# Where the high and low halves of weights and activations start in SBUF: rows placed by their byte address modulo 256

## What is computed

```python
def first_block(x, ...):
    for layer in range(2):
        h = rms_norm(x, g_mix[layer])
        x = x + (even_mixer(h, ...) if layer == 0 else odd_mixer(h, ...))   # projections in, attention, projection out
        h = rms_norm(x, g_mlp[layer])
        x = x + jnp.square(jax.nn.relu(h @ w_up[layer])) @ w_down[layer]    # 1024 -> 4096 -> 1024
    return x
# then x = x + mlstm_mixer(rmsnorm(x), ...), x = x + nsa_mixer(rmsnorm(x), ...), and a last rmsnorm
```

## The kernel before

| kind | moving, before | loaded beside it | offset before | moving, after | loaded beside it | offset after |
|---|---|---|---|---|---|---|
| narrow, h moving, 256 columns | h 192 | w 128 | 192 | h_hi 64, h_lo 0 | w_hi 128, w_lo 64 | 64 |
| MLP up L1164, 512 | h pair 192 | w_lo 128 | 192 | h pair 64 | w_lo 64 | 0 |
| MLP up L1165, 256 | h 192 | w_hi 128 | 192 | h 64 | w_hi 128 | 64 |
| MLP down, 512 | w 128 | u 64 | 192 | w_hi 128, w_lo 64 | u_hi 128, u_lo 64 | 0 |
| wide, h stationary, 512 | w 128 | h 192 | 64 | as above | h_hi 128, h_lo 64 | 0 |
| values of the last mixer (48 of the wide ones) | w 128 | h 192 | 64 | as above | h_hi 64, h_lo 0 | 192 |
| even_y stationary, 512 | w 128 | 128 | 0 | as above | y_hi 128, y_lo 64 | 0 |
| odd_y, nsa_y stationary | w 128 | 96, 64 | 224, 192 | as above | as above | 0 |
| ml_y stationary, 512 | w 128 | hi 160, lo all residues | 32, all | as above | as above | 0 |
| one chunk, w moving, h stationary, 256 | w 128 | h 192 | 64 | as above | h_hi 128, h_lo 64 | 0 |

## Time and profile before

### The profile page before, as it was taken

The page is one execution under the profiler, slowest core; times in us unless marked ns, Lnnn a source line. Parts: engine busy times, 40 slices in busy tenths (PEclk is TensorE's granted clock), DMA queues, the critical chain, the costliest instruction groups (busy, mean ns, idle before and its releaser), DMA issues.

```text
span 949.1 us, 14124 instructions
## 1 busy us (share of the span) xinstructions
PE 940.5 (99%) x5608; PEld 794.3 (84%) x5608; DVE 627.3 (66%) x1134; ACT 561.6 (59%) x926; POOL 98.3 (10%) x142
## 2 busy tenths in 40 slices
PE   9999999999999999999999999999999999999997
PEld 7777888888888777688888888999988889988876
DVE  6767687764446565568776354677479757677875
ACT  6697555553434776655554343556477547777774
POOL 0210000000000000000000007145002201311101
PEclk9999999999999999999999999999999999999999
DMA  9733455565554425146555556233333644421201
GB/s 366 311 130 129 171 222 177 183 216 177 178 203 152 169 97 178 45 138 221 190 197 187 185 212 217 90 133 134 134 133 104 229 171 178 169 99 45 90 23 45
DMA packets 22417, 152.59 MB, mean 161 GB/s; under 512 B 2512, under 2 KB 2768, under 8 KB 4944
## 3 DMA queue, kind: packets, MB, share of 16 engines
q1 hardware_dynamic: 21424, 148.25, 43.4%
q0 software_dynamic: 640, 3.15, 1.0%
q10 hardware_dynamic: 288, 0.30, 0.1%
HBM read 150.64 MB, written 1.05 MB: 160 GB/s over the span
## 4 chain that ended last, share of the span: by engine, by line
PE 96%; DVE 2%; ACT 1%; DMA 1%; issue 0%; SPq 0%; ACTq 0%; DVEq 0%
PE bank L188 20%; PE bank L190 20%; PE bank L189 20%; PE bank L1164 13%; PE bank L1165 6%; PE bank L930 2%; PE bank L2313 1%; PE bank L2322 1%; PE bank L954 1%; PE bank L2337 1%; PE bank L1600 1%; PE bank L943 1%; PE bank L760 1%; PE bank L1585 1%; PE bank L1577 1%; DMA raw<-in_chunks 1%
## 5 line engine op out<-in xcount | busy, mean ns | idle before, releaser
L158 DVE TENSOR_TENSOR w_hi_lo<-raw,w_hi_lo 128x2048 fp32r<-128x2048 f32 x121 | 277.5, 2296 | 138.2 <-ACT w_hi_lo L154 138.0
L154 ACT ACTIVATE w_hi_lo<-raw 128x2048 fp32r<-128x2048 f32 x135 | 257.6, 1911 | 108.8 <-PE bank L190 108.3
L1164 PE MATMUL bank<-h,w_hi_lo 128*128 128x512 f32 x512 | 181.2, 396 | 0.0
L1165 PE MATMUL bank<-h,w_hi_lo 128*128 128x256 f32 x512 | 144.4, 282 | 0.0
L188 PE MATMUL bank<-h,w_hi_lo 128*128 128x256 f32 x448 | 129.5, 289 | 0.1
L189 PE MATMUL bank<-h,w_hi_lo 128*128 128x256 f32 x448 | 125.2, 279 | 0.0
L190 PE MATMUL bank<-h,w_hi_lo 128*128 128x256 f32 x448 | 125.0, 279 | 0.0
L1164 PEld LDWEIGHTS bank<-h,w_hi_lo 128*128 128x128 f32 x512 | 96.2, 188 | 23.4 <-issue 0.2
L190 PE MATMUL bank<-w_hi_lo,mlp_u_lo 128*128 128x512 f32 x256 | 100.6, 393 | 0.0
L188 PE MATMUL bank<-w_hi_lo,mlp_u_hi 128*128 128x512 f32 x256 | 100.5, 393 | 0.0
L189 PE MATMUL bank<-w_hi_lo,mlp_u_hi 128*128 128x512 f32 x256 | 99.7, 390 | 0.0
(11 more groups left out here) (402 smaller groups left out, 1588.3 us busy)
## 6 DMA issues: line engine op xcount, KB each, us to landing
raw<-in_chunks SPq DMA_DIRECT2D x136, 1024.0 KB, 4.8
even_bias<-in_even POOLq DMA_DIRECT2D x8, 384.0 KB, 3.4
xres<-in_x SPq DMA_DIRECT2D x2, 512.0 KB, 5.3
raw<-in_chunks SPq DMA_DIRECT2D x2, 512.0 KB, 6.2
ml_z<-in_ml SPq DMA_DIRECT2D x1, 896.0 KB, 6.5
small<-in_small SPq DMA_DIRECT2D x1, 559.5 KB, 11.6
final_gain<-in_fnorm SPq DMA_DIRECT2D x1, 512.0 KB, 3.3
out<-final_xn SPq DMA_DIRECT2D x1, 512.0 KB, 2.6
```

The lines of the kernel that those rows point to most:

```text
L154: act.activation(w_hi[slot][:, :], raw[slot][:, :], ACT.Copy).then_inc(hi_ready, 1)
L158: dve.tensor_tensor(w_lo[slot][:, :], raw[slot][:, :], w_hi[slot][:, :].bitcast(F32), ALU.subtract).then_inc(lo_ready, 1)
L1164: pe.matmul(dst[:, :], w_hi[slot][:, cols], h[:, k, :, :], start=(k == 0), stop=False)
L1165: last = pe.matmul(dst[:, 0:S], w_lo[slot][:, cols], h[:, k, 0, :], start=False, stop=(k == KT - 1))
```

## The change

No instruction is added, removed or moved: engine by engine the program has the same instructions with the same shapes and the same waits in the same order. Only the SBUF addresses differ. The weights' ring becomes one tensor in which w_lo starts at 64 modulo 256 and w_hi at 128. h becomes a room that is read through three views: as pairs at 64 for the MLPs (`hu_hi`, `hu_lo`), as two planes at 128 and 64 where it is stationary (`h_hi`, `h_lo`), and as two planes at 64 and 0 for the mLSTM and the last mixer (`hm_hi`, `hm_lo`). Unused pads move u and y so that their high half starts at 128 and their low half at 64.

```diff
-    w_both = [sb(ctx, f"w_hi_lo{i}", [P, 2, CHUNK], F32R) for i in range(RING)]
-    w_hi, w_lo = ([w[:, x, :] for w in w_both] for x in range(2))
+    SHIFT = 16
+    W_ROW = CHUNK + 3 * SHIFT
+    W_SLOT = 2 * CHUNK + 4 * SHIFT
+    w_room = sb(ctx, "w_hi_lo", [P, RING * W_SLOT + 2 * SHIFT], F32R)
+    w_both = [w_room[:, i * W_SLOT:i * W_SLOT + 2 * W_ROW].rearrange("p (x c) -> p x c", x=2) for i in range(RING)]
+    w_hi, w_lo = ([w[:, x, 0:CHUNK] for w in w_both] for x in range(2))
...
+    sb(ctx, "pad_h", [P, 64])
...
             self.u_hi = sb(stack, f"{name}_u_hi", [P, D_FF // P, S], F32R)
+            sb(stack, f"{name}_pad_lo", [P, 3 * SHIFT])
             self.u_lo = sb(stack, f"{name}_u_lo", [P, D_FF // P, S], F32R)
...
-                pe.matmul(dst[:, :], w_hi[slot][:, cols], h[:, k, :, :], start=(k == 0), stop=False)
-                last = pe.matmul(dst[:, 0:S], w_lo[slot][:, cols], h[:, k, 0, :], start=False, stop=(k == KT - 1))
+                pe.matmul(dst[:, :], w_hi[slot][:, cols], h_pairs[:, k, :, :], start=(k == 0), stop=False)
+                last = pe.matmul(dst[:, 0:S], w_lo[slot][:, cols], hu_hi[:, k, :], start=False, stop=(k == KT - 1))
...
-    h = sb(big, "h", [P, KT, 2, S], F32R)
-    h_hi, h_lo = h[:, :, 0, :], h[:, :, 1, :]
+    PLANE = KT * S
+    h_room = sb(big, "h", [P, 2 * PLANE + 4 * SHIFT], F32R)
+
+    def plane(at):
+        return h_room[:, at:at + PLANE].rearrange("p (k s) -> p k s", k=KT)
+
+    h_pairs = h_room[:, 0:2 * PLANE].rearrange("p (k x s) -> p k x s", k=KT, x=2)
+    hu_hi, hu_lo = h_pairs[:, :, 0, :], h_pairs[:, :, 1, :]
+    h_hi, h_lo = plane(SHIFT), plane(PLANE + 4 * SHIFT)
+    hm_hi, hm_lo = plane(0), plane(PLANE + 3 * SHIFT)
...
+    sb(es, "pad_even_y", [P, 48])
     ey_hi = sb(es, "even_y_hi", [P, KT, S], F32R)
+    sb(es, "pad_even_lo", [P, 3 * SHIFT])
...
-            self.y_lo = sb(stack, "ml_y_lo", [P, ML_TILES, KW], F32R)[:, :, KW - S:KW]
+            sb(stack, "pad_ml_lo", [P, 3 * SHIFT])
+            self.y_lo = sb(stack, "ml_y_lo", [P, ML_TILES, S], F32R)
...
-                last = product(pe, dst, w_hi[slot][:, cols], w_lo[slot][:, cols], h_hi[:, k, :], h_lo[:, k, :],
+                last = product(pe, dst, w_hi[slot][:, cols], w_lo[slot][:, cols], hm_hi[:, k, :], hm_lo[:, k, :],
```

More of the change, by code:

```diff
@@ L743, in build, with __init__ @@
     class Turned:
-        def __init__(self, name, gain, banks):
-            self.gain, self.banks = gain, banks
+        def __init__(self, name, gain, banks, hi, lo):
+            self.gain, self.banks, self.hi, self.lo = gain, banks, hi, lo
             self.turned, self.hi_done, self.lo_done = (
@@ L767, in act @@
                     act.wait_ge(self.turned.sem, self.turned.at(k // 2 + 1))
-                act.activation(h[:, k, 0, :], self.spot(k), ACT.Copy, scale=self.gain[:, k:k + 1])\
+                act.activation(self.hi[:, k, :], self.spot(k), ACT.Copy, scale=self.gain[:, k:k + 1])\
                    .then_inc(self.hi_done.sem, 1)
@@ L774, in dve @@
                     dve.wait_ge(self.hi_done.sem, self.hi_done.at(k + 2))
-                dve.scalar_tensor_tensor(h[:, k, 1, :], self.spot(k), self.gain[:, k:k + 1],
-                                         h[:, k, 0, :].bitcast(F32), ALU.mult, ALU.subtract).then_inc(self.lo_done.sem, 1)
+                dve.scalar_tensor_tensor(self.lo[:, k, :], self.spot(k), self.gain[:, k:k + 1],
+                                         self.hi[:, k, :].bitcast(F32), ALU.mult, ALU.subtract).then_inc(self.lo_done.sem, 1)
     class Stats:
@@ L1294, in build @@
     mlo_at = sb(big, "mlo_stats", [P, 5, TT])
+    sb(big, "pad_stage", [P, 48])
     es = ExitStack()
@@ L1324, in build @@
     E_IN, E_OUT = FIRST["even_in"], FIRST["even_out"]
-    e_turned = Turned("ein", sm("g_mix0"), (4, 5, 6, 7))
-    m0_turned = Turned("m0in", sm("g_mlp0"), (4, 5, 6, 7))
+    e_turned = Turned("ein", sm("g_mix0"), (4, 5, 6, 7), h_hi, h_lo)
+    m0_turned = Turned("m0in", sm("g_mlp0"), (4, 5, 6, 7), hu_hi, hu_lo)
     e_norm = HeadNorm(es, "en", e_stats, 4, 5)
@@ L1334, in build @@
     ms = ExitStack()
-    o_turned = Turned("oin", sm("g_mix1"), (0, 1, 2, 3))
+    o_turned = Turned("oin", sm("g_mix1"), (0, 1, 2, 3), h_hi, h_lo)
     mlp0 = Mlp(ms, "mlp0", FIRST["mlp0"], m0_turned, e_out, m0_stats, (0, 1, 2, 3), (4, 5, 6, 7))
@@ L1396, in build @@
     oqg = sb(os_, "odd_qg", [P, 1])
+    sb(os_, "pad_odd_y", [P, 56])
     wf_hi = sb(os_, "wf_hi", [P, KT * HEADS], F32R)
@@ L1400, in build @@
     oy_hi = sb(os_, "odd_y_hi", [P, KT, S], F32R)
+    sb(os_, "pad_odd_lo", [P, 3 * SHIFT])
     oy_lo = sb(os_, "odd_y_lo", [P, KT, S], F32R)
@@ L1415, in build @@
     O_IN, O_OUT = FIRST["odd_in"], FIRST["odd_out"]
-    m1_turned = Turned("m1in", sm("g_mlp1"), (0, 1, 2, 3))
+    m1_turned = Turned("m1in", sm("g_mlp1"), (0, 1, 2, 3), hu_hi, hu_lo)
     o_sq = sb(os_, "odd_x2", [P, TT, WIDE])
@@ L1475, in __init__ @@
             self.mv = sb(stack, "ml_mv", [P, ML_HEADS, TT, 2])
+            sb(stack, "pad_ml_y", [P, 40])
             with ExitStack() as tmp:
@@ L2053, in build @@
     ls = ExitStack()
-    ml_turned = Turned("mlin", sm("ml_norm"), (4, 5, 6, 7))
+    ml_turned = Turned("mlin", sm("ml_norm"), (4, 5, 6, 7), hm_hi, hm_lo)
     mlstm = Mlstm(ls, ml_turned, mlp1, m1_stats)
@@ L2098, in __init__ @@
             self.y_hi = sb(stack, "nsa_y_hi", [P, KT, S], F32R)
+            sb(stack, "pad_nsa_lo", [P, 3 * SHIFT])
             self.y_lo = sb(stack, "nsa_y_lo", [P, KT, S], F32R)
@@ L2135, in __init__ @@
                 self.rt = [sb(tmp, f"nsa_rt{i}", [P, 2, S]) for i in range(2)]
+                sb(tmp, "pad_wg", [P, 48])
                 self.wg_hi = sb(tmp, "nsa_wg_hi", [P, KT * GW], F32R)
@@ L2267, in gates @@
                 w = slice(k * GW, (k + 1) * GW)
-                last = product(pe, bank[2][0:GW, 0:S], self.wg_hi[:, w], self.wg_lo[:, w], h_hi[:, k, :], h_lo[:, k, :],
+                last = product(pe, bank[2][0:GW, 0:S], self.wg_hi[:, w], self.wg_lo[:, w], hm_hi[:, k, :], hm_lo[:, k, :],
                                k == 0, k == KT - 1)
@@ L2367, in values_half @@
                 pe.wait_ge(self.g_step.sem, self.g_step.at(3))
-            last = wide_half(pe, c, t, bank[2 + t][:, :], h_hi, h_lo, range(part * WIDE_KT, (part + 1) * WIDE_KT),
+            last = wide_half(pe, c, t, bank[2 + t][:, :], hm_hi, hm_lo, range(part * WIDE_KT, (part + 1) * WIDE_KT),
                              part == 0, part == 1)
@@ L2925, in build @@
     ns = ExitStack()
-    nsa_turned = Turned("nsin", sm("nsa_norm"), (4, 5, 6, 7))
+    nsa_turned = Turned("nsin", sm("nsa_norm"), (4, 5, 6, 7), hm_hi, hm_lo)
     nsa = Nsa(ns, nsa_turned, mlstm, mlstm.out_stats)
```

## The result

| | before | after |
|---|---|---|
| median of 7 runs each, same chip | 950.99 us (950.82 to 951.41) | 954.18 us (954.01 to 954.39) |
| ratio, 95% interval | 1 | 1.0033 (1.0022 to 1.0045) |
| profiled execution | 950.89 us | 954.14 us |
| its span | 949.1 us | 952.3 us |
| PE busy | 940.5 us | 944.2 us |

The forecast was 933.9 us with a range of 928 to 943. The time came out 20 us above it and outside the range, on the side that had been given 0.07.

A forecast was written before the change was run, and what follows sets the result against it. TensorE's matmul count times spacing bounds the kernel. Terms of 6.0 + 6.8 + 1.7 + 3.1 + 1.0 + 0.6 - 0.2 = 19.0 us, less 2.0, give 950.9 - 17.0 = 933.9 us, range 928 to 943.

The forecast's parts named there:

- what bounds the kernel: Whole kernel: time is the number of TensorE matmuls times what each holds the engine; only the second can change.
- the floor at offset 0: 512-column matmuls in long rows at offset 0: spacing of 226.7 ns, taken as the floor.
- What comes off it: Some 500 products in the first six behind a break miss the floor: 4 ns each, 2.0 us off the gain.
- 1.7 us for MLP down: MLP down: 768 products go from offset 192 to 0, 228.9 to 226.7 ns, gaining 1.7 us.
- 2.9 + 0.2 us for wide: Wide products with h: 456 go to offset 0, gaining 2.9 us; 48 go from 64 to 192, gaining 0.2 us.
- The step that no row covers: Starts jumping by 64 between products, in both streams, taken as harmless; bounds zero and the slower rival's price.
- rival 3: Alternating starts cost, no row locks: MLP down 233.0 ns, MLP up pairs 360 ns, 957.5 us; chance 0.07.
- the narrow term: Narrow products, h moving: 1344 go from offset 192 to 64, 117.8 to 113.3 ns, gaining 6.0 us.
- the MLP up term: MLP up: 512 pairs of 512 and 256 columns go from 353.2 to 340.0 ns, gaining 6.8 us.
- Rival 2: Nothing moves, since something other than the offset sets the stages' spacings: 950.9 us; chance 0.08.
- Rival 1: Only rows of one width gain; MLP up's alternating pairs stay at 353.2 ns: 940.7 us; chance 0.15.
- rival 4: More than the floor: seams come free too, some 4100 products gain 9 us on top, 925 us; chance 0.05.

The follow-up runs named there:

- flat_a: Changed kernel with each low half at its high half's residue, so nothing jumps; offset 0 in wide products, 64 in narrow and MLP up; 943.87 us, ratio 0.9922.
- flat_64: flat_a with weights, u, y and both views of h moved to residues 64 lower, no offset changed; 944.50 us.
- flat_b: flat_a with other MLP offsets: 0 in the first MLP up, 128 in the second MLP up and second MLP down; 945.37 us.
- the sweeps: Two kernels from the changed one without jumps, with other offsets spread over MLP down, MLP up and narrow products; 951.5 and 951.92 us.

## Why the prediction was wrong, step by step

**Right: what bounds the kernel.** Time is matmuls times spacing. No wait took over in any kernel, down to a span of 935.5 us, and stages at one offset and without jumps repeat to 0.1 ns at 512 columns.

**Right: the floor at offset 0, once nothing jumps.** "Offset 0 in a long row: 226.7 ns" held as soon as nothing jumped: MLP down 226.7, and the wide rows with h 228.3 with their starts, some 1.6 ns above it, which is the kind of loss that "What comes off it" had allowed for. Of the terms 1.7 us for MLP down and 2.9 + 0.2 us for wide, flat_a has (228.9 - 226.8) x 768 = 1.6 us and 5.0 x 504 = 2.5 us.

**Wrong: "The step that no row covers".** The jump of 64 between products was "taken as harmless", with the reason that the offset within each product is kept. That reason is the step that failed. At offset 0 in every product, MLP down takes 226.8 ns without jumps, 231.1 with +64 or 128, and 233.3 with the -64 of the change. "Absolute residues did not matter" was right (flat_64) and did not bear on it, since no row had a jump. The step turned the 1.7 us of MLP down into a loss of 3.4 us and took the gain of the wide rows and of ml_y. Without jumps flat_a is 10.3 us quicker than the changed kernel, though its MLP up pairs are 1.8 us slower; the other 10.0 us to the forecast are the next two steps, 3.2 us of narrow and 6.8 of MLP up. The upper bound had been put at rival 3's price and was not let into the range; a step that the whole sum goes through, and for which no row stands, deserved more than 0.07.

**Wrong: the narrow term, 6.0 us.** One stretch at offset 64 gave 113.3 ns, two at 192 gave 117.8, and I took the difference for the offset's. The trace of before already had two stretches at 192 with 113.2 and 113.4 ns. Without jumps offset 64 is worth (117.7 - 115.7) x 672 + (117.3 - 115.2) x 672 = 2.8 us with the two stages weighed alike; with jumps it costs 1.6 us. The chunk that left offset 64 went from 113.5 to 119.9 ns, past the 117.8 of its bound, 0.3 us instead of 0.2; flat_a has 119.8 there, so this one belongs to offset 0 and not to the jump.

**Wrong: the MLP up term, 6.8 us.** The size was exactly right for another offset: 340.0 ns a pair exists, at 0 and 192. At 0 and 64, where the changed kernel has it, the pair takes 349.7, a gain of 1.8 us. The step that failed is "each half has its precedent at exactly that offset": the precedents stood in rows of one width, and a pair is not the sum of such rows (the table of offsets). Nor does 340.0 bear the sum out: its 256 columns are at offset 192, for which the prediction had 117.8 ns. That the very number appears is luck.

**The rivals.** Rival 3, the alternating start, named the mechanism. It put MLP down at 233.0 ns, and 233.3 was measured. The number is partly luck, since it was the spacing of rows at offset 64 and other jumps give 231.1; and "no row can lock" is not what the rows do, which are even at 233.3 ns. It missed the sum, 957.5 against 954.2 us, since MLP up did not take 360 ns but gained, while the narrow rows lost. Its deciding point, MLP down above 228.9 with no gain in the narrow rows, is what the trace shows. Rival 2, that nothing depends on the offset, falls with flat_b and the sweeps: the same instructions take 226.7 to 234.3 ns. Rival 1 gets its 353.2 ns wrong, and its idea that alternating lengths cannot lock falls with the 340.0. Nothing ran below 226.7 and 113.3 ns, so rival 4 has no support.

**The rule of the Trainium skill.** The same MLP down instructions take 226.7, 228.9, 231.1 or 233.3 ns, and only the addresses differ. "TensorE: Matmul & The Clock Gate", Part 2, step 1, of the Trainium skill has weight loads and the moving stream on read ports of their own, so that a load takes nothing from the running matmul; by that all of these would be equal. The traces do not agree. The rule's result, 950.9 us, would nevertheless have been nearer to the time than mine.

**Left open.** Which of two spacings a row or a stage falls into, and why a jump costs, is not settled. The cost of the two jumps adds up in MLP down (2.2 + 4.4 = 6.6 ns), but for the moving stream's -64 alone the single odd offset gives the same mean.

## What to carry to other kernels

Where back-to-back matmuls bound a kernel and shapes and counts are fixed, compare the spacings of equal matmuls before anything else: here addresses alone move the kernel between 937.3 and 954.5 us. Keep each operand of a row at one residue modulo 256 for its high and low half, and look for the offset between the moving and the loaded stream by a run for each, with the instructions in the order that the kernel has, since a mixed row is not the sum of rows of equals; here that is 0 for 512 columns, 64 for 256, and 0 with 192 for alternating ones. Before a spacing is put down to an address, look whether the same addresses show another spacing elsewhere in the trace, and do not let a gain rest on a property (here, that successive products keep their residue) that holds in every row read and that the change gives up.
